# Weight halves side by side, and three pads of 32 bytes: a split-precision block on one core

## The reference, cut to what matters

```python
for i in range(2):
    x = x + 0.5 * swiglu(rms_norm(x, ln_ffn1[i]), ffn1_w_gu[i], ffn1_w_down[i])
    h = rms_norm(x, ln_mix[i])
    x = x + (even_mixer(h, ...) if i % 2 == 0 else odd_mixer(h, ...))
    x = x + 0.5 * swiglu(rms_norm(x, ln_ffn2[i]), ffn2_w_gu[i], ffn2_w_down[i])
    x = x + sigmoid(rms_norm(x, ln_ple[i]) @ ple_w_gate[i]) * (p[i] @ ple_w_in[i])
# second block: one projection to 11 groups of columns, a convolution, an LRU, an RWKV recurrence
x = x + merge(rms_norm(x, norm1_g) @ w_in, ...) @ w_out
x = x + square(relu(rms_norm(x, norm2_g) @ mlp_w1)) @ mlp_w2
return rms_norm(x, final_g)
```

## Time and profile before

| | |
|---|---|
| median of 3 runs | 1748.44 us |
| span of the profiled execution | 1751.1 us |
| TensorE matmul busy | 1694.5 us, 14502 matmuls |
| TensorE weight load busy | 1574.0 us, 14502 loads |
| DVE busy | 1290.8 us |
| ACT busy | 995.2 us |
| granted TensorE clock, mean | 0.982 |
| read from HBM | 274.59 MB, 158 GB/s |

### The profile page before, as it was taken

How to read it: one execution, slowest core, us unless ns; L and a number is a source line. 1 busy time by engine, 2 the same in 40 slices (tenths; PEclk the granted TensorE clock), 3 DMA queues, 4 the chain that set the end, 5 groups by cost and what they waited for, 6 DMA issues and landing times.

```text
span 1751.1 us, 37772 instructions
## 1 busy us (share of the span) xinstructions
PE 1694.5 (97%) x14502; PEld 1574.0 (90%) x14502; DVE 1290.8 (74%) x2137; ACT 995.2 (57%) x1562; POOL 3.0 (0%) x9
## 2 busy tenths in 40 slices
PE   7999999999999999999999999989999999899998
PEld 6999899889999989999988999989999998798887
DVE  6777867658777887777767777877788774567776
ACT  5544655445444664445555554668877875444444
POOL 0000000000000000000000000000000000000000
PEclk9999989899999999999999999999999999999999
DMA  6555533115555445554425655545555550055554
GB/s 230 191 188 183 165 133 109 62 31 181 192 191 188 162 166 192 180 191 157 145 82 173 192 188 188 169 157 184 178 183 191 175 163 4 23 174 179 186 187 144
DMA packets 75864, 278.24 MB, mean 159 GB/s; under 512 B 8432, under 2 KB 8688, under 8 KB 75248
## 3 DMA queue, kind: packets, MB, share of 16 engines
q1 hardware_dynamic: 75168, 273.58, 47.9%
q0 software_dynamic: 592, 3.15, 0.5%
HBM read 274.59 MB, written 2.10 MB: 158 GB/s over the span
## 4 chain that ended last, share of the span: by engine, by line
PE 83%; DVE 8%; ACT 6%; issue 2%; DMA 0%; DVEq 0%; SPq 0%; ACTq 0%
PE ps L475 82%; DVE w_lo L464 2%; ACT w_hi L456 2%; PE ps L2471 1%; DVE rstd L607 1%; DVE x L943 1%; DVE h L568 1%; DVE arena L911 0%; DVE arena L915 0%; ACT L2796 0%; ACT L2780 0%; DMA x<-x_t 0%; DVE arena L656 0%; DVE a_lo L931 0%; ACT arena L2133 0%
## 5 line engine op out<-in xcount | busy, mean ns | idle before, releaser
L475 PE MATMUL ps<-h,w_hi 128*128 128x256 f32 (+1 forms) x3380 | 732.4, 307 | 0.0
L464 DVE TENSOR_TENSOR w_lo<-raw,w_hi 128x1024 fp32r<-128x1024 f32 x514 | 621.4, 1215 | 86.6 <-ACT w_hi L456 67.5
L456 ACT ACTIVATE w_hi<-raw 128x1024 fp32r<-128x1024 f32 x514 | 538.6, 1050 | 223.2 <-PE ps L475 205.6
L475 PE MATMUL ps<-h,w_lo 128*128 128x256 f32 x2026 | 583.9, 289 | 22.9 <-DVE w_lo L464 15.6
L475 PEld LDWEIGHTS ps<-h,w_hi 128*128 128x128 f32 x3380 | 554.4, 193 | 26.4
L475 PEld LDWEIGHTS ps<-h,w_lo 128*128 128x128 f32 x2026 | 390.5, 193 | 30.1 <-DVE w_lo L464 14.5
L475 PE MATMUL ps<-h_of_feed_forward,w_hi 128*128 128x512 f32 (+1 forms) x1088 | 351.5, 374 | 0.0
L475 PE MATMUL ps<-h_of_feed_forward,w_lo 128*128 128x256 f32 x1000 | 278.8, 281 | 0.8 <-issue 0.6
L896 ACT ACTIVATE arena<-ps 128x256 f32<-128x256 f32 x208 | 79.1, 382 | 267.7 <-PE ps L475 267.7
L475 PEld LDWEIGHTS ps<-h_of_feed_forward,w_hi 128*128 128x128 f32 x1088 | 198.3, 188 | 36.3
L475 PE MATMUL ps<-a_hi,w_lo 128*128 128x256 f32 x776 | 218.3, 281 | 4.2 <-DVE a_lo L931 4.2
(11 more groups left out here) (354 smaller groups left out, 1447.9 us busy)
## 6 DMA issues: line engine op xcount, KB each, us to landing
raw<-weights SPq DMA_DIRECT2D x514, 512.0 KB, 3.4
con<-shape_constants SPq DMA_DIRECT2D x1, 1618.0 KB, 10.5
x<-x_t SPq DMA_DIRECT2D x1, 1024.0 KB, 5.0
stored<-x POOLq DMA_DIRECT2D x1, 1024.0 KB, 4.8
x<-stored POOLq DMA_DIRECT2D x1, 1024.0 KB, 7.9
out_t<-arena SPq DMA_DIRECT2D x4, 256.0 KB, 2.1
arena<-p_t POOLq DMA_DIRECT2D x2, 256.0 KB, 4.1
arena<-final_gain POOLq DMA_DIRECT2D x1, 512.0 KB, 4.6
```

Source lines behind the costliest of these rows:

```text
L456: A.activation(w_hi[:, u % RING, 0:n], raw[:, u % RING, 0:n], ACT.Copy).then_inc(s_hi, 1)
L464: V.tensor_tensor(w_lo[:, u % RING, 0:n], raw[:, u % RING, 0:n], f(w_hi[:, u % RING, 0:n]), SUB)\
L475: return TE.matmul(o, lhsT, rhs, start=start, stop=stop, skip_group_check=True)
```

## The change

`w_hi` and `w_lo` become one tensor `w` of the same size. A unit's slot of 2048 floats holds, for most units, pairs: element n's rounded half at 2n and its remainder at 2n + 1. A new helper `parts_of(u, cols)` gives the two views, which step by two floats (8 bytes). The 35 units that are moving operands (the set `planar`) keep the two halves one behind the other, so their views step by one float. All readers and the two writers (`act_split`, `dve_split`) take their views from `parts_of`. Pads: the one in front of `h` shrinks by 8 floats and the one behind it grows by as many, so `h` lies 32 bytes earlier and `raw` and `w` stay where `raw` and `w_hi` were. The pad of 8 floats in front of `a_hi` goes, so `a_hi`, `a_lo` and all that is declared behind them, the arena and `h_of_feed_forward` too, lie 32 bytes earlier. `h`, `a_hi`, `a_lo`, `h_of_feed_forward` and `w` then all begin at 64 bytes past a multiple of 128. Number, order, shapes and waits of the instructions stay the same on every engine.

```diff
         x = sb("x", [P, KT, T])
-        sb("in_front_of_h", [P, 56])
+        sb("in_front_of_h", [P, 48])
         h = sbr("h", [P, KT, 2, T])
-        sb("behind_h", [P, 88])
+        sb("behind_h", [P, 96])
         raw = sb("raw", [P, RING, UNIT])
-        w_hi, w_lo = sbr("w_hi", [P, RING, UNIT]), sbr("w_lo", [P, RING, UNIT])
-        sb("in_front_of_a", [P, 8])
+        w_ = sbr("w", [P, RING, 2 * UNIT])
         a_hi, a_lo = sbr("a_hi", [P, 3, T]), sbr("a_lo", [P, 3, T])
...
+        planar = set()
+        if "even" in stages:
+            planar.add(unit_base["even"] + 26)
+        if "odd" in stages:
+            planar |= {unit_base["odd"] + 15, unit_base["odd"] + 16}
+        if "mlp" in stages:
+            planar |= set(range(unit_base["mlp"] + 2, unit_base["mlp"] + 2 * FJ2 - 4, 2))
+            planar |= {unit_base["mlp"] + 2 * FJ2 - n for n in (3, 2, 1)}
+
+        def parts_of(u, cols):
+
+            slot = w_[:, u % RING, :]
+            if u in planar:
+                return slot[:, 0:UNIT][:, cols], slot[:, UNIT:2 * UNIT][:, cols]
+            pairs_ = slot.rearrange("p (n two) -> p n two", two=2)
+            return pairs_[:, cols, 0], pairs_[:, cols, 1]
...
-                A.activation(w_hi[:, u % RING, 0:n], raw[:, u % RING, 0:n], ACT.Copy).then_inc(s_hi, 1)
+                A.activation(parts_of(u, slice(0, n))[0], raw[:, u % RING, 0:n], ACT.Copy).then_inc(s_hi, 1)
...
-                V.tensor_tensor(w_lo[:, u % RING, 0:n], raw[:, u % RING, 0:n], f(w_hi[:, u % RING, 0:n]), SUB)\
+                hi, lo = parts_of(u, slice(0, n))
+                V.tensor_tensor(lo, raw[:, u % RING, 0:n], f(hi), SUB)\
                     .then_inc(s_lo, 1)
...
-            return mm3(o, w_hi[:, u % RING, c_], w_lo[:, u % RING, c_], hi, lo, start, stop)
+            return mm3(o, *parts_of(u, c_), hi, lo, start, stop)
...
-                mm(ps[:, bank, 0:T], w_lo[:, u % RING, c_], h_[:, k, 0, :], k == 0, False)
-                last = mm(ps[:, bank, :], w_hi[:, u % RING, c_], h_[:, k, :, :].rearrange("p a t -> p (a t)"), False, k == KT - 1)
+                mm(ps[:, bank, 0:T], parts_of(u, c_)[1], h_[:, k, 0, :], k == 0, False)
+                last = mm(ps[:, bank, :], parts_of(u, c_)[0], h_[:, k, :, :].rearrange("p a t -> p (a t)"), False, k == KT - 1)
```

More of the change, by code:

```diff
@@ L528, in early_units @@
                         pe.wait_ge(s_hr, h_at[n] + k // 2 + 1)
-                    mm(ps[:, bank, 0:T], w_lo[:, u % RING, c_], src[:, k, 0, :], k == 0, False)
-                    mm(ps[:, bank, 0:T], w_hi[:, u % RING, c_], src[:, k, 0, :], False, False)
+                    mm(ps[:, bank, 0:T], parts_of(u, c_)[1], src[:, k, 0, :], k == 0, False)
+                    mm(ps[:, bank, 0:T], parts_of(u, c_)[0], src[:, k, 0, :], False, False)
             for i_, (u, bank) in enumerate(tiles):
@@ L534, in early_units @@
                         pe.wait_ge(s_h, h_at[n] + k // 2 + 1)
-                    last = mm(ps[:, bank, 0:T], w_hi[:, u % RING, k * P:k * P + P], src[:, k, 1, :], False, k == KT - 1)
+                    last = mm(ps[:, bank, 0:T], parts_of(u, slice(k * P, k * P + P))[0], src[:, k, 1, :], False, k == KT - 1)
                 last.then_inc(s_prod, 1)
@@ L624, in opening @@
                             pe.wait_ge(s_hr, h_at[n] + k // 2 + 1)
-                        mm(o, w_lo[:, u % RING, c_], h_[:, k, 0, :], k == 0, False)
-                        mm(o, w_hi[:, u % RING, c_], h_[:, k, 0, :], False, False)
+                        mm(o, parts_of(u, c_)[1], h_[:, k, 0, :], k == 0, False)
+                        mm(o, parts_of(u, c_)[0], h_[:, k, 0, :], False, False)
             for i_, (u, bank) in enumerate(tiles):
@@ L631, in opening @@
                         pe.wait_ge(s_h, h_at[n] + k // 2 + 1)
-                    last = mm(o, w_hi[:, u % RING, k * P:k * P + P], h_[:, k, 1, :], False, k == KT - 1)
+                    last = mm(o, parts_of(u, slice(k * P, k * P + P))[0], h_[:, k, 1, :], False, k == KT - 1)
                 last.then_inc(s_prod, 1)
@@ L823, in tokens_down @@
                 l_hi, l_lo = a_hi[:, j % f_.bufs, b_], a_lo[:, j % f_.bufs, b_]
-                return mm3(ps[:, q, :], l_hi, l_lo, w_hi[:, u % RING, c_], w_lo[:, u % RING, c_], False, stop)
+                return mm3(ps[:, q, :], l_hi, l_lo, *parts_of(u, c_), False, stop)
             def last_tokens_down():
@@ L1388, in pe_prog @@
                     for k in range(2):
-                        sl, c_ = (u0 + 26) % RING, slice(k * 512, (k + 1) * 512)
+                        c_ = slice(k * 512, (k + 1) * 512)
                         last = mm3(ps[:, (5, 4)[tb], :], h_hi[:, 3 + k, blk(tb)], h_lo[:, 3 + k, blk(tb)],
-                                   w_hi[:, sl, c_], w_lo[:, sl, c_], k == 0, k == 1)
+                                   *parts_of(u0 + 26, c_), k == 0, k == 1)
                 last.then_inc(s_prod, 1)
@@ L2039, in pe_prog @@
                             last = mm3(ps[:, 4 + tb, 0:T], h_hi[:, k, blk(tb)], h_lo[:, k, blk(tb)],
-                                       w_hi[:, u % RING, c_], w_lo[:, u % RING, c_], k == 0, k == 7)
+                                       *parts_of(u, c_), k == 0, k == 7)
                     last.then_inc(s_prod, 1)
```

## The result

The changed kernel takes 1775.35 us (median of 4 runs, 1772.56 to 1776.17); the kernel before, timed beside it, 1747.82. The ratio is 1.0154 [1.014, 1.0168]: 27.5 us slower, where 1705 us, 43 less, was predicted. The profiled executions differ by less: spans of 1773.3 and 1751.1 us, 22.2 apart. In the runs on record an execution's time lies about 2 us above its span (1775.16 against 1773.3 for this one), so the profiled execution of the kernel before, taken ahead as 2.7 us above its median, is by this estimate some 4.7 above it; that is nearly all of the 5.3 between 27.5 and 22.2.

A forecast was written before the change was run, and what follows sets the result against it. TensorE's dense matmul streams were taken as the bound. Gains of 10.3, 13.2, 0.9, 2.4, 10.6 and 5.8 us sum to 43.2; 1748.4 - 43.2 = 1705.2, predicted as 1705 us, range 1676 to 1757.

The forecast's parts named there:

- the load's share goes and the stream's own stays: TensorE's fp32r streams: 8-byte load steps cut 256-column matmuls to 112.2 ns, 512-column to 224.3; 43.2 us gained in all.
- plain-float rows: Profile rows of plain-float matmuls, taken as nearest case: load alone 111.3 ns, 256 columns 215.5 ns, no loss.
- the load's share: Fp32r matmuls: 4.9 of the 9.3 ns lost per 256 columns put down to the weight load beside them.
- Locked in collision: Rival: load and columns at equal pace and start meet every step; about 43 us slower, 1792 us; chance 0.13.
- No change: Rival: ports independent, the 9 ns belong to fp32r itself or to the switch of weights; 1748 us; chance 0.14.
- full relief: Rival: all stream losses were the overtaking and go, 63 us; 1685 us; chance 0.16 for below 1690.
- the part of it up to 1745: Forecast case that only a rest of the gain comes, 1728 to 1745 us; chance 0.08.
- The load that fetches twice: Slow bound: the 8-byte step makes a load take 222 ns, +865 us over about 8240 matmuls; chance 0.04.
- ACT's slowed write: Slow bound: ACT's 1056 ns split doubles, 506 us of ACT time; about 1748 + 40 plus some 28; chance 0.05.
- Pads: Activations moved 32 bytes earlier: zero for paired units, +-1.6 us for planar units in `mlp`, +-40 us as ends.
- DVE at nothing: DVE's split writing and reading with an 8-byte step costs nothing, by 0.692 us dense against 0.69 stepped.
- ACT at nothing: ACT's split writing with an 8-byte step costs nothing, staying at 1056 ns, by DVE's row as nearest.

The follow-up runs named there:

- pairs_old_pads: The changed kernel with the three pads of the kernel before put back (56, 88 and 8 floats); 1772.75 us, ratio 1.0142.
- pairs_up_only: The kernel before, old pads, with pairs only for the way-up units of the gated feed-forward stages; 1755.21 us, ratio 1.0042.
- act_twice: The kernel before with ACT's split of each unit cut into two instructions (256 and 768 floats); 1749.4 us, ratio 1.0014.
- quads: The changed kernel with two tiles and both halves interleaved, so a load steps by 16 bytes; 5-tile units split as 6; one run, 2689.73 us.
- planar_narrow: The kernel before, but in the gated stages' way down two matmuls of each three move only 32 columns; one run, 1755.23 us.
- pairs_narrow: The changed kernel, but in the gated stages' way down two matmuls of each three move only 32 columns; one run, 1781.05 us.

## Why the prediction was wrong

**The bound was read rightly.** TensorE's dense streams set the time, the distance between starts was the thing to ask for, and the loss of the changed kernel lies where 35 of the 43 us of gain were expected: in the gated stages and `second`.

**The step that failed** is "I take it that the load's share goes and the stream's own stays". It made 112.2 ns of a 256-column matmul, 224.3 of one of 512, and -43.2 us in the sum; measured are 119.6 ns, 238 and +22.2 us. With this step alone, the pads left as they were (`pairs_old_pads`), it is 120.8 ns, 233 and +24.7 us in the median. Two things were wrong in it. The plain-float rows have two streams in step, but their load is contiguous; the pace of a load with a step stood in no row, and the prediction took it as 111 ns. It is 117, so the load alone forbids 112. And the 4.9 ns called the load's share, an inference from two spacings, rested on the idea that unequal pace does the harm. `pairs_up_only` shows the opposite sign: with the load at the columns' pace the 512 columns lose 3 to 4 ns more. That the two streams "stay apart" after one wait is shown by no run. Of the two ends, the one where a load fetches twice as much (222 ns) is near what a step of 16 bytes gives (233). For 8 bytes the truth lay just on the slow side of no change, and there the prediction held only its rivals. Both signs that it named against itself came: a 256-column distance above 117 ns, and ACT above 1100.

**The rivals.** *Locked in collision* had the right side, named the mark, a distance above 118, and priced the time at 1792, the nearest of all. That is luck: its cause is not borne out, since the loss stays at the three offsets tried. *No change* fell, and *full relief* and the part of it up to 1745 with it. The load that fetches twice and ACT's slowed write had the right sign and far too large a size: +7 ns instead of +111, and +90 instead of +1056.

**Pads.** Taken as zero for paired units. The totals with old and new pads (ratios 1.0142 and 1.0154) can't be told apart, so for the whole this holds, though inside it two effects cancel in part. For a kernel without pairs, which the prediction did not forecast, the same pads cost 10.6 us, inside the +-40 that the earlier trace rows gave as ends. `mlp`'s way down gained 2.5 ns, 384 x 2.5 = 1 us, within the +-1.6.

**DVE** at nothing was right (1222 and 1223 ns). **ACT** at nothing was wrong in size, +90 ns a split, and nearly right in effect: TensorE's wait for the splits stayed at 15.5 us, and in `act_twice` +192 ns cost 0.1% of the whole.

The Trainium skill (SBUF — State Buffer, "Door 1: The DMA port swizzle") has two hits on a 16-byte line keep full speed. The runs agree for DVE's split only. With two hits ACT's split takes 1146 ns instead of 1056 and the load 117 instead of 110; with one hit (`quads`) DVE takes 1985, ACT 2003 and the load 233. The measurement decides: two hits are nearly full speed, and in a stream whose bound is the load, nearly is a loss. The Trainium skill's rule of two independent read ports (TensorE: Matmul & The Clock Gate, "Step-by-step: what each phase is for"), weighed in the prediction, does not hold to the letter either: whether the load beside them has a step changes the pace of the columns by 1 to 2% (`pairs_up_only`).

**Open.** Why two hits cost the load 7 ns rather than nothing or 111 was not settled, nor by what mechanism it holds up the columns, nor why the relative place counts, nor what sets the way down to about 120 ns. That it is visits to memory is a reading that goes with 4, 8 and 16 bytes; no run counted them.

## What to carry to other kernels

Where each matmul has its own weight load and few columns, the load is a second bound just under the first: here 7 ns on 110 went with 1.4% of the whole. In such a kernel keep stationary operands contiguous, and put interleaving, if it must be, on operands that only DVE uses, whose split lost nothing at 8 bytes. Change layout and place in separate steps: here the pads alone cost 10.6 us, and changed together with the pairs they could not be told from them. When a prediction rests on a pace that no row shows, a stretch that isolates it (here, two of three matmuls cut to 32 columns) is worth more than a split of losses between two spacings.

## What the runs showed of the hardware that was not expected

- A load of 128 columns takes about 110 ns at a step of 4 bytes, 117 at 8 and 233 at 16 (`planar_narrow`, `pairs_narrow`, `quads`).
- ACT's write of 1024 elements takes 1056, 1146 and 2003 ns at these steps; DVE's split 1222, 1223 and 1985.
- The offset between moving and stationary operands modulo 128 bytes changes the whole by up to 0.7% on contiguous weights, and the way down and the way up have different favourites. At 64 bytes, 256 columns of `second` run at 113.3 ns instead of 118.3.
